# Two-layer transformer kernel: twelve of 22 up-projection steps as seven half-block products with weight sums made by DMA

## The reference

```python
D_MODEL, SEQ, D_FF, CONV_W = 1024, 512, 2816, 3

def conv_ffn(h, w_up, conv_w, conv_b, w_down):
    S = h.shape[1]
    u = h @ w_up                                   # 512x1024 @ 1024x5632
    up = jnp.pad(u, ((0, 0), (CONV_W - 1, 0), (0, 0)))
    u = conv_b + sum(conv_w[j] * up[:, j:j + S] for j in range(CONV_W))
    gate, val = jnp.split(u, 2, axis=-1)
    return (jax.nn.silu(gate) * val) @ w_down

x = x + mixer(rms_norm(x, norm_mix[layer]))
x = x + conv_ffn(rms_norm(x, norm_ffn[layer]), w_up, conv_w, conv_b, w_down)
```

## Time and profile before

| | |
|---|---|
| median of 3 runs | 1191.81 us (1190.55 to 1193.16) |
| the profiled execution's own time | 1191.57 us |
| span of its records | 1189.8 us |
| PE / DVE / ACT / POOL busy | 99% / 73% / 52% / 29% of the span |
| granted TensorE clock | 0.998 of full speed over the span |
| DMA moved | 174.54 MB, mean 147 GB/s |

### The profile page before, as it was taken

How to read it: one execution, slowest core, us unless ns; L and a number is a source line. 1 busy time by engine, 2 the same in 40 slices (tenths; PEclk the granted TensorE clock), 3 DMA queues, 4 the chain that set the end, 5 groups by cost and what they waited for, 6 DMA issues and landing times.

```text
span 1189.8 us, 18961 instructions
## 1 busy us (share of the span) xinstructions
PE 1174.8 (99%) x6874; PEld 999.6 (84%) x6874; DVE 862.7 (73%) x1502; ACT 617.0 (52%) x1033; POOL 348.5 (29%) x429
## 2 busy tenths in 40 slices
PE   9999999999999999999999999999999999999998
PEld 7768886778888888888999887988888888888998
DVE  6588968945766566579897898855766666579986
ACT  6554337855434333345565789945534334335563
POOL 0633547830042522211000366730042421211000
PEclk9999999999999999999999999999999999999999
DMA  7555352253398785436554110053387574326553
GB/s 281 182 187 199 142 202 65 73 142 106 106 238 238 199 217 184 175 109 211 186 160 138 62 37 2 1 125 107 106 192 179 156 172 130 106 71 208 176 173 127
DMA packets 51555, 174.54 MB, mean 147 GB/s; under 512 B 4720, under 2 KB 6128, under 8 KB 41504
## 3 DMA queue, kind: packets, MB, share of 16 engines
q1 hardware_dynamic: 36352, 127.51, 31.3%
q0 software_dynamic: 15136, 46.14, 16.3%
HBM read 171.50 MB, written 52.47 MB: 188 GB/s over the span
## 4 chain that ended last, share of the span: by engine, by line
PE 93%; DVE 3%; ACT 2%; issue 1%; POOL 0%; DVEq 0%; ACTq 0%; POOLq 0%
PE ps L2554 28%; PE ps L2556 27%; PE ps L2555 27%; PE ps L2269 3%; PE ps L2253 3%; PE ps L2069 1%; PE ps L2520 1%; PE ps L2110 1%; PE ps L2237 1%; PE ps L2140 1%; ACT probs L977 1%; DVE w_lo L1705 1%; DVE xT L1725 0%; PE ps L2121 0%; ACT w_hi L1148 0%
## 5 line engine op out<-in xcount | busy, mean ns | idle before, releaser
L2554 PE MATMUL ps<-h_hi,w_hi 128*128 128x512 f32 x704 | 274.4, 390 | 0.0
L2555 PE MATMUL ps<-h_lo,w_hi 128*128 128x512 f32 x704 | 273.9, 389 | 0.0
L2556 PE MATMUL ps<-h_hi,w_lo 128*128 128x512 f32 x704 | 273.9, 389 | 0.0
L1394 DVE TENSOR_TENSOR w_lo<-raw,w_hi 128x2048 fp32r<-128x2048 f32 (+1 forms) x62 | 123.0, 1984 | 118.3 <-ACT w_hi L887 118.3
L1216 ACT ACTIVATE cv<-u_in,vec 128x512 f32<-128x512 f32 x88 | 71.2, 816 | 180.4 <-DVE u_in L1835 178.3
L887 ACT ACTIVATE w_hi<-raw 128x2048 fp32r<-128x2048 f32 (+1 forms) x72 | 121.8, 1692 | 69.1 <-PE ps L2556 69.1
L2554 PEld LDWEIGHTS ps<-h_hi,w_hi 128*128 128x128 f32 x704 | 132.2, 188 | 27.6 <-issue 0.7
L2556 PEld LDWEIGHTS ps<-h_hi,w_lo 128*128 128x128 f32 x704 | 132.2, 188 | 27.6
L2555 PEld LDWEIGHTS ps<-h_lo,w_hi 128*128 128x128 f32 x704 | 132.2, 188 | 27.3
L762 POOL TENSOR_TENSOR v<-act 128x256 f32<-128x256 f32 x16 | 43.3, 2707 | 345.2 <-DVE act L1872 345.2
L2554 PE MATMUL ps<-a_hi,w_hi 128*128 128x256 f32 (+1 forms) x440 | 138.9, 316 | 2.2 <-DVE a_lo L1709 2.2
(11 more groups left out here) (276 smaller groups left out, 2421.6 us busy)
## 6 DMA issues: line engine op xcount, KB each, us to landing
raw<-in_f_up SPq DMA_DIRECT2D x44, 1024.0 KB, 5.0
w_sums<-in_f_w_down POOLq DMA_DIRECT2D x22, 1024.0 KB, 8.7
w_sums<-in_f_w_down POOLq DMA_DIRECT2D x44, 512.0 KB, 9.0
raw<-w_sums SPq DMA_DIRECT2D x44, 512.0 KB, 4.2
raw<-in_a_in_wide SPq DMA_DIRECT2D x12, 1024.0 KB, 6.1
raw<-in_f_w_down SPq DMA_DIRECT2D x22, 512.0 KB, 3.9
raw<-in_f_w_down SPq DMA_DIRECT2D x22, 256.0 KB, 4.0
bias_tiles<-bias_rows SPq DMA_DIRECT2D x1, 4096.0 KB, 27.0
```

What stands on the lines that cost most here:

```text
L1394: dve.tensor_tensor(w_lo[:, s, 0:n], raw[:, s, 0:n], w_hi[:, s, 0:n].bitcast(F32), ALU.subtract)\
L2554: pe.matmul(dst, s_hi, m_hi, start=start, stop=False)
L2555: pe.matmul(dst, s_hi, m_lo, start=False, stop=False)
L2556: return pe.matmul(dst, s_lo, m_hi, start=False, stop=stop)
```

## The change

In layer 0 the steps 5 to 8 and in layer 1 the steps 1 to 8 are made as seven products of half blocks (features halved, tokens halved, gate and value as the two rows of the result). Each of the seven is 2 channel tiles x 4 blocks x 3 matmuls of 256 columns, 168 matmuls a step, and needs its own 128 x 1024 piece of weights. PE makes the seven products into three banks that change from step to step; some products are added onto a bank that ACT has copied out between two of them. Sums of features (`t_hi`, `t_lo`) are made once per layer. Weight sums are made in HBM by DMAs from POOL, which are placed among its work in the stages before.

```
+SEVENS = ((5, 6, 7, 8), (1, 2, 3, 4, 5, 6, 7, 8))
...
+            def copy_up(l, z, h):
+                src = f_up[l, SEVENS[l][z]]
+                if h:
+                    pool.dma_start(w_more[l][z], src[0], max_dma_last_dim=8192).then_inc(up_sums, 16)
+                else:
+                    pool.dma_start(w_two[l][z].rearrange("p (a n) -> p a n", a=2), src[:, :, 0:D].rearrange("s p n -> p s n"))\
+                        .then_inc(up_sums, 16)
+            def two_up(l, z):
+                if z == 0:
+                    pool.wait_ge(up_sums, sums_made(l, 2))
+                pool.dma_start(w_two[l][z], f_up[l, SEVENS[l][z], 1], accum_op=ALU.add, max_dma_last_dim=8192)\
+                    .then_inc(up_sums, 16)
+            def three_up(l, z):
+                if z == 0:
+                    pool.wait_ge(up_sums, sums_made(l, 3))
+                pool.dma_start(w_more[l][z][:, 0:D], w_two[l][z][:, D:2 * D], accum_op=ALU.add).then_inc(up_sums, 16)
+            def four_up(l, z):
+                if z == 0:
+                    pool.wait_ge(up_sums, sums_made(l, 4))
+                pool.dma_start(w_more[l][z][:, D:2 * D], w_more[l][z][:, 0:D], accum_op=ALU.add).then_inc(up_sums, 16)
```

`sums_made(l, n)` is the count at which the first n DMAs of every changed step of the layer have landed. Where POOL issues them:

```
             for u in range(POOL_LO[0], POOL_LO[1]):
+                j = u - POOL_LO[0]
+                if j < 8:
+                    copy_up(0, j // 2, j % 2)
                 pool_lo(u)
-                copy_weights(0, 1 + u - POOL_LO[0])
+            for z in range(4):
+                two_up(0, z)
...
             for u in range(UNITS):                      # layer 0's attention
                 normed(0, u)
...
+                if 5 <= u < 9:
+                    three_up(0, u - 5)
+                if 12 <= u < 16:
+                    four_up(0, u - 12)
...
             for w in range(Q_HALVES):                   # queries of layer 1
...
+                copy_up(1, w, 0)
...
                 for w in (2 * (T + t), 2 * (T + t) + 1):
                     key_tails(w)
+                    copy_up(1, w - 2 * T, 1)
...
             for u in range(UNITS):                      # layer 1's attention
                 normed(1, u)
                 if u and next_split(u - 1):
                     keys_lo(*next_split(u - 1))
+                if 1 <= u < 9:
+                    two_up(1, u - 1)
+                elif 10 <= u < 14:
+                    three_up(1, 2 * (u - 10))
+                    three_up(1, 2 * (u - 10) + 1)
+                elif 15 <= u < 19:
+                    four_up(1, 2 * (u - 15))
+                    four_up(1, 2 * (u - 15) + 1)
+                elif u >= 19:
+                    copy_weights(1, u - 19)
```

The start of the feed-forward part, ahead of `root_of_mean` on ACT and `token_rstd` on DVE, and ahead of `rbc` on ACT:

```
+                gained_features(n // 2)
+                sum_hi(n // 2, 0)
+                sum_hi(n // 2, 1)
                 root_of_mean(n_next)
...
                 total_squares(n_next)
+                sums_of_features(n // 2)
+                sum_lo(n // 2, 0)
+                sum_lo(n // 2, 1)
                 token_rstd(n_next)
...
+                    if i == 0:
+                        unit_hi(l, 0)
+                        unit_hi(l, 1)
+                        sum_hi(l, 2)
+                        sum_hi(l, 3)
                         sc.wait_ge(bc_ok, l + 1)
...
+                unit_lo(l, 0)
+                unit_lo(l, 1)
+                sum_lo(l, 2)
+                sum_lo(l, 3)
+                chain.then_wait(dve.memset(u_in[:, :, 0:2], 0.0))
                 dve.wait_ge(rbc_ok, l + 1)
```

A changed step on PE, on ACT and on DVE (m is the step's first piece):

```
+                    for j, (b, moving) in enumerate(((0, 0), (2, 3), (0, 4), (1, 1), (0, 5), (2, 2), (0, 6))):
+                        pe.wait_ge(w_lo_done, U_UP[l] + 2 + m + 1)
...
+                        if z > 1 and j == 0:
+                            pe.wait_ge(f_snap, LANDED + SNAP_AT[l][i - 2] + 5)
+                        if z > 1 and j in (1, 3):
+                            pe.wait_ge(f_in, IN_AT[l][i - 2] + {1: 3, 3: 1}[j])
+                        if j in (2, 4, 5, 6):
+                            pe.wait_ge(f_snap, LANDED + SNAP_AT[l][i] + {2: 1, 4: 3, 5: 2, 6: 4}[j])
...
+                def seven_step(i):                       # ACT
+                    m, behind = unit_of(l, i), i - 1 in SEVENS[l]
+                    if behind:
+                        keep(i - 1, 6)
+                        tap2(i - 1, 2)
+                        tap2(i - 1, 3)
+                    keep(i, 0)
+                    unit_hi(l, m + 4)
+                    if behind:
+                        silu(i - 1)
+                    keep(i, 1)
+                    unit_hi(l, m + 5)
+                    keep(i, 2)
+                    unit_hi(l, m + 6)
+                    unit_hi(l, m + 7)
+                    keep(i, 4)
+                    unit_hi(l, m + 8)
+                    unit_hi(l, m + 9)
+                    tap2(i, 0)
+                    tap2(i, 1)
+                    unit_hi(l, m + 10)
...
+                def seven_step(i):                       # DVE
+                    if behind:
+                        second_row(i - 1)
+                        unit_lo(l, m + 3)
+                        taps(i - 1, (0, 1))
+                    unit_lo(l, m + 4)
+                    if behind:
+                        taps(i - 1, (2, 3))
+                    unit_lo(l, m + 5)
+                    first_row(i, 0)
+                    if behind:
+                        gated(i - 1)
+                    unit_lo(l, m + 6)
+                    second_row_sum(i)
+                    unit_lo(l, m + 7)
+                    unit_lo(l, m + 8)
+                    first_row(i, 1)
+                    unit_lo(l, m + 9)
```

396 lines of the change are left out of this document (295 added, 101 removed).

## The result

The changed kernel takes 1279.96 us (median of 4 runs, 1278.06 to 1281.87), the kernel before 1191.41 us beside it: 1.0741 times as long, with a 95% interval of 1.0721 to 1.0762. The prediction was 1218 us, within 1189 to 1230. It had the sign and missed 62 of the 88.5 us, so the time lies far outside its range.

What follows compares the result with a forecast made beforehand. PE, busy 99% of the span, was taken as the bound through its matmuls' number and spacing. Terms -19.7 + 5.7 + 2.0 + 7.6 + 3.1 + 25 + 3 = +26.7 us on 1191.57 gave 1218 us, range 1189 to 1230.

Steps and rivals of the forecast that it cites:

- part 8: Feed-forward parts: smaller splits in plain steps, postponed gate_sums and down sums, and seven piece loads a changed step cost nothing.
- part 6: Layer 1's attention: POOL waits for adding DMAs at about 203 GB/s; 18 us behind unit 10, 7 behind unit 15, +25 us.
- Part 1: PE's own work: a changed step takes 20.07 us instead of 21.71; -19.7 us over twelve steps.
- Part 2: Changed steps: a closed chain of DVE and ACT takes 20.8 us, 0.75 more than PE needs; +5.7 us.
- Part 3: Step ahead of each layer's first changed one: the third weight piece is split late on DVE; +2.0 us for both layers.
- Part 4: Start of the feed-forward part: sums of features delay root transposes by 2.0 us and step 1 by 1.8; +7.6 us both layers.
- Part 5: Layer 1's query tails: eight more DMA issues on POOL at 0.57 us each, less idle time; +3.1 us.
- Part 7: Layer 0's attention: four two_up make the first bias tiles some 5 us late, about half covered by PE's work; +3 us.
- rival B: Changed steps: DVE and ACT become the bound, the chain taking a microsecond above 20.8; 10 us more, 1228 us; chance 0.15.
- Rival A: Accumulates keep up, as doubling is per row: two_up takes 3.1 us, 1195 us in all, or 1192 at 2.8; chance 0.23.

Runs made afterwards that it cites:

- the mended order: Edits to the order inside the steps; five such edits on the changed kernel without POOL's DMAs took 1188.74 us, 0.9975 of the kernel before.

## Why the prediction was right and wrong

The result lies outside the range because of part 8 and part 6 above all. Part by part:

*Part 1* (PE's spacing, -19.7) was right: 20.1 us a changed step, once nothing disturbs it.

*Part 2* (the closed chain, +5.7) was right in mechanism and size: 20.7 us a step as changed, 20.1 with one high part moved out of the chain. What it left out is POOL: `gate_sums` beside DVE add 1.4 us of waiting to each of two steps of layer 1, and without POOL's DMAs the lower clock adds 1.5 us to the second of them. The profile of before shows POOL's sums beside DVE, but not in a step where DVE had no room.

*Part 3* (the step ahead, +2.0) was mis-sized for layer 1. In layer 0 PE waits 0.45 us (1 forecast). In layer 1 the step ahead is step 0, whose DVE work starts late behind `rbc`, and PE waits 6.0 us for `w_lo` (1 forecast). I used step 3 of layer 0 for both.

*Part 4* (start, +7.6) was right in mechanism and 2 us too high: PE waits 1.3 and 1.6 us at the root transposes and 2.1 (layer 0) or 0.5 us (layer 1) ahead of step 1, 5.5 us in all; with the sums of features behind `rbc`, these are gone.

*Part 5* (query tails, +3.1) had the mechanism and too small a price for an issue among POOL's operations. One tail with `kv_lo` and its copy now follows the other after 4.10 us instead of 3.15:

```profile
698.90 0.85 POOL L933 TENSOR_TENSOR rope_tmp<-act,rope 128x256 f32<-128x256 f32 x1
...
703.00 0.85 POOL L933 TENSOR_TENSOR rope_tmp<-act,rope 128x256 f32<-128x256 f32 x1
```

With its issue a tail thus costs some 0.95 us more and not 0.57 (the operations behind an issue last a little longer too, 0.85 instead of 0.74 us), and the eight tails together take 5.2 us more (27.9 against 22.7). The eight issues of the key stage, which this part didn't count, cost 0.5 us: there it holds that the stage is PE's own. The stage of the table lost 6.4 us in all.

*Part 6* (layer 1's attention, +25) had the mechanism, and the two waits it named came to 14.9 and 8.5 us on POOL, 15.9 and 8.0 on PE (18 and 7 forecast). Its rate was right: 43.1 us for eight `two_up` of 1.05 MB is 195 GB/s, and the plain copies made these waits nearly vanish. The statement of the Trainium skill ("Collectives: The Full Stack", the part "Why ReduceScatter is half of AllGather") that an adding DMA is slower agrees in direction: adding was worth 26 us. The term is 18.5 us short, and PE's waits, 35.7 us in all, account for 10.7 of these: 9.7 at unit 1, where POOL waits 8.7 us for sixteen copies, which I took to be landed, although 16.8 MB were issued behind one another in the stage before, and 2.1 in three short ones, less 1.1 at the two places named. The other 7.8 us aren't waits of PE; the lower clock behind the waits (window means 0.64 and 0.71) is the cause that the rows show, but no run tells how much of the 7.8 is its own.

*Part 7* (layer 0's attention, +3) is 9.7 us short. I had the first bias tile 5 us late with half of it hidden; DVE waited 7.7 us and then 3.4 for the next tile. With plain copies the stage is still 8.5 us longer, with `two_up` earlier, among the first projections, 3.5 us.

*Part 8* is the step that failed most. I wrote that the postponed down copies and sums, and seven loads a step, cost nothing, called the loads "the weakest cover here", and gave them no bound of their own: late loads stood in the range only through rival B, at 10 us. Without these DMAs the kernel takes 24.4 us less. My check was of throughput (a load is 1.2 us, a slot is free 5 us ahead). The measure that counts is how long a load takes to land behind a burst: 16.0 us for the copies of step 0, 10.3 to 18.0 us for the loads issued while they are under way, against 5.2 us for a load twice as large before. The Trainium skill ("DMA: Bandwidth & Descriptors", "Queues, rings and completion order") has each DMA engine take turns between the queues it has work for. By that rule, as an estimate, a load beside POOL's DMAs lands at about half speed; 10.3 us and more, against 4.1 without POOL's DMAs, is that and more, so the rule alone doesn't give the size.

Rival A (the accumulates keep up) is refuted by 195 GB/s (its 82 ns a row come to 84.5 by the earlier trace rows, which leaves its price at 3.1 us). Rival B named the right victim, the chain of DVE and ACT beside late loads, at 10 us. By the table of stages the 63 us between the sum (26.7) and the spans (90.2) are 9.7 of part 7, 3.3 of part 5, 18.5 of part 6, and 7.3 and 24.2 in the up steps. Without POOL's DMAs the up steps took 240.6 and 246.5 us, so 7.3 and 14.7 of these are part 8. The rest, 9.5 us in layer 1, is about what 5 us of part 3, 3 of `gate_sums` and 3 of lower clock come to, less 1 us that the start cost less than forecast.

What stays open: why the six copies, moved away, gave only 4 us in total when the stage that held them gave 9 (the first stage's 3.3 us above all); and how the 9.5 us in the last down projection divide.

## What to carry to other kernels

Where a change doubles the loads of a loop and halves their size, cost them by landing time behind the largest burst that another queue can put in front of them, not by bytes over bandwidth; and let an unknown of that kind widen the range. With the same bytes, DMAs issued one by one at marks of the consumer's progress, together with the mended order, left 11 of the 88 us; the order alone was worth some 10. Before an engine is given the last free microsecond of a step, look who shares its port and what stands in its closed chain: one copy moved behind another in ACT's order was worth 10 us.

## What the runs showed of the hardware

- An adding DMA from memory to memory with rows of 8 KB ran at 195 GB/s (eight of 1.05 MB in 43.1 us), as the 2 KB rows did at 203: the row's length didn't help. Eight of 0.52 MB with rows of 4 KB took 26.9 us from the first issue, 156 GB/s, for which no run shows the cause. Its issue holds POOL 0.80 to 1.36 us in this attention, a plain one 0.59.
- DVE's low parts with two SBUF inputs took 3.44 us for two beside POOL's sums, 2.35 without; both engines were slowed (POOL 1.6 us for an operation of 0.74).
- A 512 KB load on SyncE's queue landed in 4.1 us (median) without POOL's DMAs, and in 10.3 to 18.0 us while six copies of 1 MB that POOL had issued in 3 us were under way.
- PE's granted clock fell to window means of 0.64 to 0.87 where PE had idled for 5.5 to 16 us, in the attention and in the first changed steps of layer 1, and stayed low for part of the work behind.
